# A one-core decoder layer on Trainium2: three places of the mixer's order moved, and two PSUM banks exchanged

## What is computed

```python
ua, va, qb, kb, vb, qc, kc, vc, gl = split(xn @ w_in)          # eight pieces of 512 columns, then 3 x 1024 gate logits
y_a = gelu(ua) * (tril(w_s) @ rms_norm(gelu(va), g_v) + b_s)   # branch A: spatial gating, 4 groups, chunks of 128 tokens
y_b = rms_norm(diff_attention(qb, kb, vb), subln_g) * 0.8      # branch B: 4 heads, two softmax maps each
y_c = stick_breaking_attention(qc, kc, vc)                     # branch C: 8 heads
g = sigmoid(gl)
merged = g[0] * (y_a @ w_up_a) + g[1] * (y_b @ w_up_b) + g[2] * (y_c @ w_up_c)
h = x + merged @ w_out
x = h + grouped_moe(rms_norm(h))                               # 16 experts, 2 for each token
```

## Time and profile before

| | |
|---|---|
| time, median of 3 runs | 532.65 us (532.55 to 533.38) |
| profiled execution: time, span | 533.18 us, 531.4 us |
| mean granted TensorE clock | 0.965 |
| busy: PE, PEld | 494.1 us (93%), 313.4 us (59%) |
| busy: DVE, ACT, POOL | 242.5 us (46%), 176.6 us (33%), 15.2 us (3%) |
| read from HBM | 142.83 MB, 271 GB/s over the span; 419 to 423 GB/s in nearly every slice of the experts' part |
| chain that ended last | PE 72%, DMA 13%, DVE 6%, ACT 5% |

### The profile page before, as it was taken

One profiled execution on the slowest core, in us unless ns is written; L12 is line 12 of the kernel. 1 busy time (PEld: TensorE's weight loads), 2 busy tenths in 40 slices (PEclk: granted clock), 3 DMA queues, 4 the chain that ended last, 5 costly groups with the idle time before them and its releaser, 6 DMA issues.

```text
span 531.4 us, 7968 instructions
## 1 busy us (share of the span) xinstructions
PE 494.1 (93%) x3276; PEld 313.4 (59%) x3276; DVE 242.5 (46%) x393; ACT 176.6 (33%) x258; POOL 15.2 (3%) x29
## 2 busy tenths in 40 slices
PE   4999999969989999999988999999999898988993
PEld 2997998748757888888876534333333242423341
DVE  6757777556533529445647823151314040413143
ACT  2744555754690425355136210110111010200113
POOL 6500000000000000000000000000000000000000
PEclk9999999979985999999998899999999998999997
DMA  8994444440440066192969379999999999999921
GB/s 290 339 336 160 160 159 158 159 158 1 159 158 0 2 231 244 51 389 71 426 241 427 136 302 422 422 421 422 421 419 421 422 422 422 421 423 421 422 120 80
DMA packets 34236, 144.25 MB, mean 271 GB/s; under 512 B 2145, under 2 KB 4209, under 8 KB 21922
## 3 DMA queue, kind: packets, MB, share of 16 engines
q1 hardware_dynamic: 33666, 142.62, 68.0%
q0 software_dynamic: 544, 1.26, 0.8%
HBM read 142.83 MB, written 1.05 MB: 271 GB/s over the span
## 4 chain that ended last, share of the span: by engine, by line
PE 72%; DMA 13%; DVE 6%; ACT 5%; issue 2%; SPq 1%; DVEq 0%; ACTq 0%
PE bank L1368 26%; PE bank L1609 23%; DMA ring<-in_moe_w 13%; PE bank L1355 10%; PE bank L1620 2%; PE bank L1600 2%; DVE ring_lo L799 1%; PE bank L1491 1%; PE bank L1492 1%; DVE work L1280 1%; DMA work<-in_norm_mix_gain 1%; PE bank L1326 1%; PE bank L1466 1%; ACT diff L617 1%; PE bank L1678 1%
## 5 line engine op out<-in xcount | busy, mean ns | idle before, releaser
L1609 PE MATMUL bank<-ring,work 128*32 128x512 f32 x1536 | 171.9, 599 | 7.2 <-DMA ring<-in_moe_w 6.4
L1609 PEld LDWEIGHTS bank<-ring,work 128*32 128x32 f32 x1536 | 47.5, 110 | 116.5 <-issue 102.3
L799 DVE TENSOR_TENSOR ring_lo<-ring,w_hi 128x2048 fp32r<-128x2048 f32 x38 | 86.5, 2295 | 25.6 <-ACT w_hi L560 25.6
L560 ACT ACTIVATE w_hi<-ring 128x2048 fp32r<-128x2048 f32 x37 | 70.3, 1909 | 70.3 <-PE bank L1368 42.6
L1368 PE MATMUL bank<-w_hi,x_hi 128*128 128x512 f32 x144 | 39.4, 395 | 0.4 <-DVE work L850 0.4
L1280 DVE SCALAR_TENSOR_TENSOR work<-bank,st,work 128x512 f32<-128x512 f32 x8 | 9.0, 1126 | 65.0 <-PE bank L1609 65.0
L1368 PE MATMUL bank<-w_hi,x_lo 128*128 128x512 f32 x144 | 38.6, 390 | 0.0
L1368 PE MATMUL bank<-ring_lo,x_hi 128*128 128x512 f32 x144 | 38.5, 390 | 0.0
L1368 PEld LDWEIGHTS bank<-w_hi,x_hi 128*128 128x128 f32 x144 | 26.5, 188 | 6.8 <-issue 1.4
L1368 PEld LDWEIGHTS bank<-w_hi,x_lo 128*128 128x128 f32 x144 | 27.0, 188 | 5.7
L1368 PEld LDWEIGHTS bank<-ring_lo,x_hi 128*128 128x128 f32 x144 | 27.0, 188 | 5.7
(11 more groups left out here) (281 smaller groups left out, 597.2 us busy)
## 6 DMA issues: line engine op xcount, KB each, us to landing
ring<-in_moe_w SPq DMA_DIRECT2D x96, 1024.0 KB, 14.6
ring<-in_w_in SPq DMA_DIRECT2D x13, 2048.0 KB, 8.1
ring<-in_w_out SPq DMA_DIRECT2D x2, 2048.0 KB, 10.9
ring<-in_w_in SPq DMA_DIRECT2D x2, 1024.0 KB, 9.1
ring<-in_w_up_b SPq DMA_DIRECT2D x1, 2048.0 KB, 7.4
ring<-in_w_up_c SPq DMA_DIRECT2D x1, 2048.0 KB, 7.4
ring<-in_w_up_a SPq DMA_DIRECT2D x1, 2048.0 KB, 8.1
h_sb<-in_x SPq DMA_DIRECT2D x2, 512.0 KB, 4.0
```

What stands on the lines that cost most here:

```text
L560: act.activation(hi(q), raw(q), ACT.Copy).then_inc(w_hi_ready, 1)
L799: dve.tensor_tensor(lo(q), raw(q), hi(q).bitcast(F32), ALU.subtract).then_inc(w_lo_ready, 1)
L1609: ins = pe.matmul(bank[cols, dst, :], lhsT[:, k, first + j * STRIP:first + (j + 1) * STRIP], rhs[e][:, k, :], start=(k == 0), stop=(k == n ...
```

## The change

Three steps move in `TIMELINE`. v's two copies become a step of their own, `va_out`, behind the logits of heads 0 and 1. Branch B's `b_done` goes behind the values of heads 0 and 1, and the splits that were part of v's second step (high split of unit 16, low split of unit 15) go behind `b_done` as a step `splits`. The spatial products, `a_mix`, go from in front of the first up projection to between the two gate units of set 1, and write banks 6 and 7 in place of 4 and 5; the semaphores that guard these banks are exchanged to match. The rounding of branch A's result moves one set later.

```diff
     for q in range(3):
         TIMELINE += [("c_sums", 2 * q), ("c_sums", 2 * q + 1), ("c_scores", 2 * q + 2), ("c_scores", 2 * q + 3),
...
+            TIMELINE += [("va_out", 0)]
...
+            TIMELINE += [("b_done", 0), ("splits", 2 * 6 + 1)]
...
@@ scalar
+            def splits(q):
+                split_hi(q + 3)
+
             def proj(c, half):
-                split_hi(2 * c + half + 3)
+                if (c, half) != (6, 1):
+                    splits(2 * c + half)
...
             def ups(s):
                 split_hi(set_unit(s, 2) + 3)
-                if s == 1:
+                if s == 2:
                     act.wait_ge(a_ready, TT)
...
@@ vector
+            def proj_out(c, b):
+                dve.wait_ge(proj_done, 2 * c + b + 1)
+                dve.tensor_copy(proj_dst(c, b), bank_view(c, b)).then_inc(pj_taken[b], 1)
+
+            def splits(q):
+                split_lo(q + 2)
+
             def proj(c, half):
-                split_lo(2 * c + half + 2)
+                if (c, half) == (6, 1):
+                    return
+                splits(2 * c + half)
                 by_rows = PROJ[c] in BY_ROWS
                 for b in range(2):
                     if (half if by_rows else b == half) and (b or PROJ[c] in (UA, VA)):
-                        dve.wait_ge(proj_done, 2 * c + b + 1)
-                        dve.tensor_copy(proj_dst(c, b), bank_view(c, b)).then_inc(pj_taken[b], 1)
+                        proj_out(c, b)
+
+            def va_out(_):
+                for b in range(2):
+                    proj_out(6, b)
...
-                                      bank[:, SC + a, :].rearrange("p (g t) -> p g t", t=P), ALU.mult)\
+                                      bank[:, TR + a, :].rearrange("p (g t) -> p g t", t=P), ALU.mult)\
...
             def ups(s):
                 split_lo(set_unit(s, 2) + 2)
-                if s == 2:
+                if s == 3:
                     dve.wait_ge(y_hi_done["A"], 1)
...
@@ tensor
             def a_mix(_):
                 pe.wait_ge(a_vn, TT)
-                pe.wait_ge(c_z, CH)
+                pe.wait_ge(y_lo_done["C"], CH // 2)
                 for a in range(TT):
                     for g in range(NG):
-                        dst = bank[:, SC + a, g * P:(g + 1) * P]
+                        dst = bank[:, TR + a, g * P:(g + 1) * P]
...
                     elif s == 1:
-                        pe.wait_ge(a_ready, TT)
+                        pe.wait_ge(c_z, CH)
...
                 elif s == 1:
-                    pe.wait_ge(y_lo_done["C"], CH // 2)
+                    pe.wait_ge(a_ready, TT)
```

More of the change, by code:

```diff
@@ L122, in trunk @@
         TIMELINE += [("c_sums", 2 * q), ("c_sums", 2 * q + 1), ("c_scores", 2 * q + 2), ("c_scores", 2 * q + 3),
-                     ("c_logits", 2 * q), ("c_logits", 2 * q + 1), ("c_keep", 2 * q + 2), ("c_keep", 2 * q + 3)]
+                     ("c_logits", 2 * q), ("c_logits", 2 * q + 1)]
         if q == 0:
-            TIMELINE += [("proj", (6, 1)), ("b_done", 0)]
-        else:
-            TIMELINE += [("proj", (7, q - 1))]
-        TIMELINE += [("c_values", 2 * q), ("c_values", 2 * q + 1)]
+            TIMELINE += [("va_out", 0)]
+        TIMELINE += [("c_keep", 2 * q + 2), ("c_keep", 2 * q + 3), ("proj", (6, 1) if q == 0 else (7, q - 1)),
+                     ("c_values", 2 * q), ("c_values", 2 * q + 1)]
+        if q == 0:
+            TIMELINE += [("b_done", 0), ("splits", 2 * 6 + 1)]
     TIMELINE += [("c_sums", 6), ("c_sums", 7), ("c_logits", 6), ("c_logits", 7), ("gates", (0, 0)),
-                 ("c_values", 6), ("c_values", 7), ("a_gelu", 0), ("a_norm", 0), ("gates", (0, 1)),
-                 ("a_mix", 0), ("ups", 0)]
+                 ("c_values", 6), ("c_values", 7), ("a_gelu", 0), ("a_norm", 0), ("gates", (0, 1)), ("ups", 0)]
     for s in range(1, SETS):
-        TIMELINE += [("gates", (s, 0)), ("gates", (s, 1))]
+        TIMELINE += [("gates", (s, 0))]
+        if s == 1:
+            TIMELINE += [("a_mix", 0)]
+        TIMELINE += [("gates", (s, 1))]
         if s == SETS - 1:
@@ L685, in merged_turn @@
                        .then_inc(merged_hi_ready, 1)
-            STEPS = {"proj": lambda i: proj(*i), "b_scores": b_scores, "b_turn": b_turn, "b_values": b_values,
-                     "b_norm": b_norm, "b_done": b_done, "c_keep": c_keep, "c_logits": c_logits,
+            STEPS = {"proj": lambda i: proj(*i), "splits": splits, "b_scores": b_scores, "b_turn": b_turn,
+                     "b_values": b_values, "b_norm": b_norm, "b_done": b_done, "c_keep": c_keep, "c_logits": c_logits,
                      "c_values": c_values, "a_gelu": a_gelu_, "a_norm": a_norm, "gates": lambda i: gates(*i),
@@ L1016, in outs @@
                         low_rows(0, a)
-            STEPS = {"proj": lambda i: proj(*i), "ws_turn": ws_turn, "b_scores": b_scores,
-                     "b_combine": b_combine, "b_values": b_values,
+            STEPS = {"proj": lambda i: proj(*i), "splits": splits, "va_out": va_out, "ws_turn": ws_turn,
+                     "b_scores": b_scores, "b_combine": b_combine, "b_values": b_values,
                      "b_norm": b_norm, "b_done": b_done, "c_scores": c_scores, "c_keep": c_keep,
```

## The result

The changed kernel took 519.26 us in the median (518.1 to 520.25, 4 runs) beside 533.01 us of the kernel before (532.55 to 533.89, 4 runs). The ratio is 0.9747, interval 0.9721 to 0.9773, which is 12.1 to 14.9 us less. A second series of the same kernel (`after_again`, 6 runs) gave 0.9772, interval 0.9745 to 0.98, which is 10.7 to 13.6 us less. The forecast was 522.1 us, in a range of 517.9 to 526.

The account below looks back on a forecast made before the run. The prediction took TensorE's own order in the mixer, with waits of 5.0 and 2.6 us, to set the time. Gains of 5.8 + 4.8 = 10.6 us off 532.65 gave 522.1 us, range 517.9 to 526.

Parts of the forecast that it names:

- The sum: Whole change: 5.8 us before the gates plus 4.8 us from there to the end of gates(1,1), together 10.6 us.
- the first term: From v's second half to the gates' first matmul: gain 5.8 us.
- Branch B's turn, 5.8 forecast: Transposes no longer wait for v's copy; VectorE's chain limits the gain; gates start at 134.3 in place of 140.09.
- the new gap: TensorE waits 1.6 us before the gates' first matmul, in place of 5.0 us before the transposes.
- The spatial products, 4.8 forecast: From the gates' start to the end of gates(1,1): 8.8 us gain without clock loss, less 4.0 us.
- the clock's price: Clock falls 4.2 us into the products: 1.9 us there and 2.1 us in gates(1,1), together 4.0 us.
- the row: Router's trace row: matmuls began at 282.18, clock fell from about 286.4, read as 4.2 us into 16-column matmuls.
- the clock holds through the products: Rival at the spatial products: no clock loss there, gain 14.6 us, 518.1 us; chance 0.16.
- 7.1 us for u's first half: In the mixer, u's first half starts at 114.24 in place of 121.35, before VectorE limits the gain.
- the gap of 1.4 us before the gates drops the clock: Rival at the gates, forecast with a 1.6 us gap: gates at half rate, +2.1 us, 524.2 us; chance 0.10.
- the end was not set elsewhere: Denies the rival that the experts' stream has a floor of its own, 532.65 us; chance 0.02.
- the slower case: Rival: after falling at the products, the clock stays low; 538 us for a 30 us low stretch; chance 0.04.

Follow-up runs that it names:

- mix_only: Spatial products moved between the two gate units of set 1, in banks 6 and 7, against the kernel before; 527.04 us, ratio 0.9905.
- turn_only: Changed kernel with v's copies and branch B's turn changed, but spatial products, banks and semaphores as in the kernel before; 525.99 us, ratio 0.9877.
- copy_only: Against turn_only: v's copies still early, but branch B's transposes ahead of the first values, as in the kernel before; 526.37 us, ratio 0.9873.
- ua_first: Against the changed kernel: VectorE's copy of u's second half put ahead of the low split of unit 17; 520.01 us, ratio 0.9742.

## Why the prediction was right

**The whole.** The sum was 10.6 us. In the profiles, from the end of v's second unit to the end of `gates(1, 1)`, the kernel before takes 184.07 - 109.70 = 74.37 us and the changed one 171.17 - 107.33 = 63.84: 10.53 us less. That this is the sum to 0.1 us is in part luck: the first term came out 0.4 us above its forecast and the second 0.4 below. What the first series measured above it, 12.1 to 14.9 us, holds in its profiled execution 2.37 us from ahead of the change, and `after_again` and `mix_only` showed that such a start comes and goes without the change. The second series, 10.7 to 13.6, still has its middle 1.6 us above the sum. Whether that too is the start, or a small gain of another place, the traces don't settle.

**Branch B's turn, 5.8 forecast.** The gates begin 24.22 us after v's second unit, 30.39 before: 6.2 us. `turn_only` by itself measured 5.4 to 7.8. Its steps held: u's first half came 4.42 us after v's (4.54 forecast), VectorE capped the rest, and the new gap was 1.42 us (1.6). Its next scores began at 113.27, which is 1.5 us behind u's first half (forecast 1.7). That VectorE's chain is the cap was shown twice over: `copy_only` has its gates only 0.3 us later with u's first half 1.4 us later, and `ua_first` closes the gap by a change on VectorE alone. The forecast gave the credit to branch B's turn as a whole; the copies alone bring all but 0.3 us of it.

**The spatial products, 4.8 forecast.** From the gates' start to the end of `gates(1, 1)` it was 43.98 us before and is 171.17 - 131.55 = 39.62 after: 4.4 us. `mix_only` measured 3.9 to 6.2. The mis-sized term is the clock's price: it fell 3.5 us into the products, not 4.2, so these took 8.76 us (8.5 forecast) and `gates(1, 1)` 7.92 (7.5). Against 6.64 and 5.44 at the full clock that is 2.1 + 2.5 = 4.6 us, forecast 4.0. In `after_again` it fell 3.1 us in, in `mix_only` 3.8, in `ua_first` 4.4: where it falls varies from one execution to the next, by more than this term is off. In the kernel before it fell 1.7 us in, soon after the 2.6 us wait, and stayed low for 13.6 us (156.7 to 170.3) in place of 10.2 (158.0 to 168.2); so the wait's end gave part of the gain through the clock too, as the forecast's sum has it. That 4.2 us came so near is luck as well. The forecast read the row as a fall within the router's 16-column matmuls, but by the same row these end at 282.18 + 3.72 = 285.90, and the clock fell at 286.4, in the wider matmuls behind them; and in the first profile of the changed kernel the router's matmuls brought no fall at all. That the clock fell inside the products without a gap ahead of it is no chance of one execution: it did so in all four profiles that have them in this order behind dense work.

**The rivals.** That the clock holds through the products (518.1) is refuted by the window 158.00:163.20 at 0.50, though the first series' 519.26 lies nearer to it than to 522.1; the traces and not the time decide here. By the Trainium skill, TensorE: Matmul & The Clock Gate, section "HAM oscillation — how this bites in real kernels", idle gaps lower the clock. For the products the trace disagrees: the clock fell with TensorE busy 3.50 of 3.50 us. Elsewhere it agrees: in the kernel before, the clock fell at 112.3, within the 5.0 us wait of the transposes, and stayed low until 119.1; this stretch is gone once the wait is.

```profile
112.00:118.80 6.80, 4.09 (x17) 2.87 (x18) 4.83 (x6) 2.73 (x4) 0.00 (x0) 0.52 0.73 280
```

The forecast didn't name this loss, but its 7.1 us for u's first half hold it: TensorE took 121.35 - 114.71 = 6.64 us from the transposes to there, and the 4.54 us put in its place come from full-clock rows. So 5.0 us of the 7.1 were the wait and 2.1 the clock, and VectorE's chain capped both together. That the gap of 1.4 us before the gates drops the clock (524.2) did not happen in either profile of the changed kernel. The experts' part moved whole, so the end was not set elsewhere; the clock came back within 5 us of dense work, so the slower case didn't come.

**What stays open.** One profile of `copy_only` had the low stretch at the products last 17.1 us where `turn_only`, which has the same order there, had 13.6; why the clock's return varies so was not tried. And of the fall itself the runs show before and in what work it comes, not what the chip counts. Whether branch B's turn moved alone would gain anything was not run.

## What to carry to other kernels

When TensorE waits for a copy, look at what stands ahead of it in the copying engine's queue: a result that is complete should leave PSUM ahead of steps that still wait for a third engine. Then ask which chain caps the gain; here it was VectorE's own, with its waits for ScalarE, so moving TensorE's work as well brought no more than 0.3 us, and the rest of the stall came back as a shorter wait further on. The run of products alternating with one-row matmuls cost the dense work behind it as well: spread such matmuls among dense ones, or join the one-row bias matmuls into one wide one, and price them with the clock that they leave behind. The time of one launch here moves by up to 2 us by its start alone, so read a gain of that size from one stretch of two traces, and look whether the clock was the same in both.

## What the runs showed of the hardware

- A 128-column float32 product alternating with a one-row bias matmul took 0.415 us each at 2.4 GHz and 0.72 at 1.2; four products in a row took 0.27 each behind one wide bias matmul, and 32 in a row 0.22. The bias matmul over 512 columns took 1.05 us, also 0.26 for 128 columns. By this comparison, alternating them cost some 0.15 us for each matmul at the full clock.
- 7.06 us of small 128-row float32 matmuls left the clock at 1.00; 3.1 to 4.4 us of products alternating with one-row matmuls, with no idle time, were followed by its fall in all four profiles with this order. Spread among matmuls of 512 columns, the same 16 left it at 1.00.
- The stretch at 1.2 GHz that began in the products lasted 10.2 us in three of these four profiles and 6.8 in `ua_first`.
- The first 16 matmuls of the mixer took 3.8 us in six profiles and 2.2 in six, and the profile's granted clock reads 1.00 in both cases. Two profiles of the changed kernel differ by 1.75 us at the end of v's second unit for it.
